# Down projections with six and seven seven-product blocks instead of five and five

## The chip, the cores and the metric

One core of a Trainium2 chip runs the whole program. The metric is the device time of one execution in microseconds. Before the change three runs took 2659.90, 2660.24 and 2660.72 us; the median is 2660.24.

## The reference

One decoder layer in float32 on 256 tokens of width 2048. It is a feed-forward part, a token mixer (a state-space branch and a windowed attention branch), and a second feed-forward part, each with a layer norm behind it:

```python
def swiglu(x, w_gate, w_up, w_down):
    return (jax.nn.silu(x @ w_gate) * (x @ w_up)) @ w_down

h = layer_norm(ALPHA * h + 0.5 * swiglu(h, ffn1_w_gate, ffn1_w_up, ffn1_w_down), ln1_g, ln1_b)
h = layer_norm(ALPHA * h + hybrid_mixer(h, ...), ln2_g, ln2_b)
h = layer_norm(ALPHA * h + 0.5 * swiglu(h, ffn2_w_gate, ffn2_w_up, ffn2_w_down), ln3_g, ln3_b)
```

The hidden width is 5632. The change touches the multiplication by `w_down` (5632 x 2048), which is done twice.

## The kernel before, in words

**Precision.** Every operand of a large product is split in two fp32r parts, high and low, and a product is three matmuls of 128 rows, 128 tokens and 512 columns: high by high, high by low, low by high (`three`, L900 to L904). The weights are split when they arrive: ScalarE copies a landed slab into `w_hi` (L1346), VectorE subtracts to get `w_lo` (L1795). A slab is two tiles of 128 weight rows by 512 columns, 512 KB. There are four landing buffers and four split buffers. SyncE issues the load of slab n when the low part of slab n-4 is done; ScalarE splits slab n when PE has finished slab n-4.

**The down projection.** The output's 2048 columns are done in two halves, j = 0 and 1, each of two column chunks c = 0 and 1. The 5632 rows are 22 k-pairs. Each half runs over the 22 pairs in `DOWN_ORDER[j]`, and each pair has one slab for each c; so a half has 44 slabs, numbered l = 0 to 43. An ordinary slab is 12 matmuls. The slabs of the next half go on counting as 44, 45 and so on in what follows. The projection of the first feed-forward part is "down 1" (f = 1), the other "down 2" (f = 2).

**Seven-product blocks.** For the pairs in `DOWN_SEVEN` the two slabs are multiplied as one 2x2 block product with seven products instead of eight: 21 matmuls instead of 24 (`seven_products`). For this a block needs
- mixed rows: four combinations of the tokens' tiles, in a tile of d_s[q] (high and low). VectorE adds and subtracts (`mixed_down`, L1987 to L1993), ScalarE makes the high part (L1456), VectorE the low part (`mixed_low`, L2019). They are made once, in the first half, and used in both halves;
- sums of the weights: four VectorE operations on the landed slabs (`block_sums`, L2027 to L2033), which need both slabs landed. ScalarE makes the high parts of the sums, VectorE their low parts (`t_low_parts`, L2039, L2042).

Products of a block go to two sets of four PSUM banks: the half's own banks, and the other half's banks (aux). When the last block of a half is done, ScalarE copies one aux bank (`copy_one_down`, L1532), and VectorE collects the rest into the residual (`collect_down`, L2117 to L2125). For j = 0 this stands at the start of the second half, ahead of its first slab's split, and PE waits for the banks; for j = 1 it stands ahead of slab 30 of that half. Own banks of the first half are evacuated at slabs 3 and 4 of the second (L2134, with statistics, L1849).

**Order.** Each engine runs its own list, written out slab by slab (`down` in the blocks of tensor, scalar and vector). In the first half VectorE also has, at slabs 10, 12, 14 and 16, the residual's rows: one operation each in down 1 (L2153), two of twice the length in down 2 (L1879, L1881, which read `rows`). Before the change the mixed tiles are made at slabs 11, 13, 15, 17 and 19, their low parts two slabs later, the blocks stand at slabs 22, 26, 30, 34 and 38 of the first half and 8, 12, 16, 20 and 24 of the second. The gains and biases of the last layer norm (`last_rows`, 2 MB) are loaded by GpSimd once PE has finished slab 23 of the second half of down 2; their place is that of pair 7, whose tiles lie where `last_rows` goes.

Of the kernel before, what the change touches and what calls it, by code (L numbers as in the profile page):

```python
# [26 lines left out]
P = 128  # L27
# [59 lines left out]
DOWN_SEVEN = (11, 13, 15, 17, 19)  # L87
DOWN_ORDER = (tuple(range(22)), (0, 1, 2, 3, 11, 4, 13, 5, 15, 6, 17, 7, 19, 8, 9, 10, 12, 14, 16, 18, 20, 21))
# [3 lines left out]
ALL_BLOCKS = UP_BLOCKS + 2 * len(DOWN_SEVEN)  # L92
# [110 lines left out]
def down_block(f, j, q):  # L203
    return (f - 1) * ALL_BLOCKS + UP_BLOCKS + j * len(DOWN_SEVEN) + q
# [68 lines left out]
def build_decoder_layer(nc, x, positions, ffn1_w_gate, ffn1_w_up, ffn1_w_down, ln1_g, ln1_b, w_in, conv_w, conv_b,  # L273
# [20 lines left out]
    with ctx:  # L294
# [15 lines left out]
        def placed(name, shape, dt, at):  # L310
# [72 lines left out]
               for k, at in enumerate((88, 92, 108, 112, 116))]  # L383
# [364 lines left out]
        def _(pe):  # L748
# [209 lines left out]
            def down_seven_block(f, j, l, own, aux):  # L958

                s = DOWN_ORDER[j][DOWN_SLABS[j][l][0]]  # L960
                q = DOWN_SEVEN.index(s)

                def rows_of(k, t):
                    return tuple(m[:, 2 * s + k, t * P:(t + 1) * P] for m in (g_hi, g_lo))

                if j == 0:
                    pe.wait_ge(mix_out, (f - 1) * MIXED + len(SEVEN) + q + 1)
                seven_products(down_block(f, j, q), slab_no(f"down{f}", j, l), l, l + 1, rows_of, d_s[q], "down",
                               own, aux, q == 0, q == len(DOWN_SEVEN) - 1)

            def down(f):

                for j in range(2):
# [5 lines left out]
                    for l, (p, c) in enumerate(DOWN_SLABS[j]):  # L979
                        if j == 1 and l >= 44 - HALVED:  # L980
                            break
                        if j == 0 and l == 3:
                            turn_hidden(f, NC_F - 1, (NC_F - 1) % 2)
                        s = DOWN_ORDER[j][p]
                        if s in DOWN_SEVEN:
# [351 lines left out]
        def _(act):  # L1337
# [189 lines left out]
            def copy_one_down(f, j):  # L1527

                act.wait_ge(t_used, down_block(f, j, len(DOWN_SEVEN) - 1) + 1)
# [4 lines left out]
            def down(f):  # L1534
                for j in range(2):
                    for l, (p, c) in enumerate(DOWN_SLABS[j]):
# [3 lines left out]
                        if j == 0 and l in (13, 15, 17, 19, 21):  # L1540
                            mixed_high(f, len(SEVEN) + (l - 13) // 2)
                        if (j, l) == (1, 0):
                            copy_one_down(f, 0)
                        if (j, l) == (1, 30):
                            copy_one_down(f, 1)
                        if s in DOWN_SEVEN and c == 1:
# [242 lines left out]
        def _(dve):  # L1789
# [216 lines left out]
            def mixed_down(f, q):  # L2006

                s = DOWN_SEVEN[q]
                if q == 0:
                    dve.wait_ge(gt_out, 2 * chunk_no(f, NC_F - 1))  # L2010
                    dve.wait_ge(t_rest, 2 * ((f - 1) * ALL_BLOCKS + UP_BLOCKS))
                at = slice(2 * s, 2 * s + 2)
# [126 lines left out]
            def down(f):  # L2139
                phase = f"down{f}"  # L2140
                for j in range(2):
                    for l, (p, c) in enumerate(DOWN_SLABS[j]):
# [23 lines left out]
                        if (j, l) == (1, 30):  # L2166
                            collect_down(f, 1)
                        n = down_block(f, j, DOWN_SEVEN.index(s)) if s in DOWN_SEVEN else None
                        if n is not None and c == 0:
                            dve.wait_ge(t_rest, n * 2)  # L2170
                            if s == DOWN_SEVEN[0]:
                                dve.wait_ge(mix_out, f * MIXED)
# [460 lines left out]
```

## Time and profile before

| | |
|---|---|
| median of 3 runs | 2660.24 us (2659.90 to 2660.72) |
| span of the profiled execution | 2657.8 us |
| PE | 2633.9 us busy, 99% |
| VectorE (DVE) | 1997.8 us busy, 75% |
| ScalarE (ACT) | 1371.5 us busy, 52% |
| down 1, first and second half | about 484 to 602 and 602 to 718 us |
| down 2, first and second half | about 2409 to 2526 and 2526 to 2642 us |
| HBM | 193 GB/s over the span |

The profile is of one execution; its span runs from its first to its last instruction, and the runs' times have some 2.4 us more. In the rows, L12 is line 12 of the kernel, PE is TensorE's matmul side, and a row such as "w_lo<-land,w_hi" names the tile written and the tiles read. A matmul's row shows 0.39 us because it contains the pipeline's latency; the distance between two starts is the time that one costs.

### The profile page before, as it was taken

How to read it: one execution, taken by the hardware profiler on the slowest of the kernel's cores; microseconds unless marked ns; L12 is line 12 of the kernel's file. 1: busy time of each engine (PE TensorE's matmuls, PEld its weight loads, DVE VectorE, ACT ScalarE, POOL GpSimd, SP SyncE). 2: the span in 40 equal slices, each digit the busy share in tenths (PEclk: the TensorE clock that was granted, in tenths of full speed). 3: DMA queues.
4: the chain of work that ended last, by engine and by line, in shares of the span. 5: the costliest groups of instructions: out<-in, count | busy, mean ns of one | idle time of the engine just before them, and what ended most of it. 6: DMA issues, size and time to landing. Idle time of an engine off the chain costs nothing.

```text
span 2657.8 us, 36761 instructions
## 1 busy us (share of the span) xinstructions
PE 2633.9 (99%) x12570; PEld 2187.7 (82%) x12570; DVE 1997.8 (75%) x2402; ACT 1371.5 (52%) x1710; POOL 129.6 (5%) x170
## 2 busy tenths in 40 slices
PE   9999999999999999999999999999999999999997
PEld 7888888888887788888888888888888888888886
DVE  6999997688666665677777765444789999977986
ACT  4555555455444554566555554444365555554553
POOL 1000000000000000211111100000000000000000
PEclk9999999999999999999999999999999999999999
DMA  7666666666655546665655565667666666666664
GB/s 224 199 197 202 193 198 213 211 201 196 204 173 148 153 150 198 206 181 180 179 177 174 180 180 166 190 190 248 203 209 198 194 206 192 202 204 230 209 208 171
DMA packets 286467, 513.96 MB, mean 193 GB/s; under 512 B 19664, under 2 KB 53120, under 8 KB 284320
## 3 DMA queue, kind: packets, MB, share of 16 engines
q1 hardware_dynamic: 279824, 485.03, 58.5%
q0 software_dynamic: 4880, 25.36, 2.6%
q10 hardware_dynamic: 1664, 2.26, 0.2%
q8 instruction: 61, 1.00, 0.2%
q14 instruction: 38, 0.31, 0.0%
HBM read 506.23 MB, written 6.36 MB: 193 GB/s over the span
## 4 chain that ended last, share of the span: by engine, by line
PE 95%; DVE 3%; ACT 1%; issue 0%; DMA 0%; ACTq 0%; POOLq 0%; POOL 0%; SPq 0%; DVEq 0%
PE acc L798 13%; PE acc L800 13%; PE acc L799 13%; PE acc L902 5%; PE acc L904 5%; PE acc L903 5%; PE acc L884 5%; PE acc L886 5%; PE acc L885 5%; PE spare L902 4%; PE spare L904 4%; PE spare L903 4%; PE spare L885 3%; PE spare L884 3%; PE spare L886 3%; PE spare L767 2%
## 5 line engine op out<-in xcount | busy, mean ns | idle before, releaser
L1795 DVE TENSOR_TENSOR w_lo<-land,w_hi 128x1024 fp32r<-128x1024 f32 (+1 forms) x956 | 1151.1, 1222 | 495.8 <-ACT w_hi L1346 488.0
L1346 ACT ACTIVATE w_hi<-land 128x1024 fp32r<-128x1024 f32 (+1 forms) x956 | 976.4, 1029 | 909.4 <-PE acc L800 324.1
L798 PE MATMUL acc<-w_hi,a_hi 128*128 128x512 f32 (+1 forms) x1168 | 443.9, 380 | 1.1 <-DVE w_lo L1795 1.1
L800 PE MATMUL acc<-w_hi,a_lo 128*128 128x512 f32 (+1 forms) x1168 | 428.8, 367 | 0.0
L799 PE MATMUL acc<-w_lo,a_hi 128*128 128x512 f32 (+1 forms) x1168 | 427.5, 366 | 0.0
L798 PEld LDWEIGHTS acc<-w_hi,a_hi 128*128 128x128 f32 x1168 | 220.3, 189 | 44.9 <-issue 10.1
L800 PEld LDWEIGHTS acc<-w_hi,a_lo 128*128 128x128 f32 x1168 | 220.2, 189 | 37.5
L799 PEld LDWEIGHTS acc<-w_lo,a_hi 128*128 128x128 f32 x1168 | 220.6, 189 | 36.5 <-issue 3.6
L884 PE MATMUL acc<-w_hi,a_hi 128*128 128x512 f32 x560 | 220.0, 393 | 0.7 <-DVE w_lo L1795 0.7
L886 PE MATMUL acc<-w_hi,a_lo 128*128 128x512 f32 x560 | 218.3, 390 | 0.0
L885 PE MATMUL acc<-w_lo,a_hi 128*128 128x512 f32 x560 | 217.8, 389 | 0.0
L884 PE MATMUL spare<-w_hi,a_hi 128*128 128x512 f32 x400 | 156.5, 391 | 0.0
L886 PE MATMUL spare<-w_hi,a_lo 128*128 128x512 f32 x400 | 155.7, 389 | 0.0
L885 PE MATMUL spare<-w_lo,a_hi 128*128 128x512 f32 x400 | 155.7, 389 | 0.0
L884 PEld LDWEIGHTS acc<-w_hi,a_hi 128*128 128x128 f32 x560 | 105.1, 188 | 23.0 <-DVE w_lo L1795 0.9
L886 PEld LDWEIGHTS acc<-w_hi,a_lo 128*128 128x128 f32 x560 | 105.1, 188 | 22.3
L885 PEld LDWEIGHTS acc<-w_lo,a_hi 128*128 128x128 f32 x560 | 105.2, 188 | 21.3
L902 PE MATMUL spare<-w_hi,g_hi 128*128 128x512 f32 x292 | 114.0, 390 | 0.6 <-DVE w_lo L1795 0.6
L902 PE MATMUL acc<-w_hi,g_hi 128*128 128x512 f32 x292 | 113.7, 389 | 0.0
L904 PE MATMUL spare<-w_hi,g_lo 128*128 128x512 f32 x292 | 113.6, 389 | 0.0
L904 PE MATMUL acc<-w_hi,g_lo 128*128 128x512 f32 x292 | 113.6, 389 | 0.0
L903 PE MATMUL spare<-w_lo,g_hi 128*128 128x512 f32 x292 | 113.6, 389 | 0.0
(393 smaller groups left out, 4302.7 us busy)
## 6 DMA issues: line engine op xcount, KB each, us to landing
land<-w_in SPq DMA_DIRECT2D x232, 512.0 KB, 3.8
land<-ffn_w_gate SPq DMA_DIRECT2D x176, 512.0 KB, 3.9
land<-ffn_w_up SPq DMA_DIRECT2D x176, 512.0 KB, 4.2
land<-ffn_w_down SPq DMA_DIRECT2D x176, 512.0 KB, 4.8
land<-w_ssd_o SPq DMA_DIRECT2D x64, 512.0 KB, 4.2
land<-w_in SPq DMA_DIRECT2D x132, 128.0 KB, 2.3
land<-w_attn_o SPq DMA_DIRECT2D x32, 512.0 KB, 4.2
land<-w_out SPq DMA_DIRECT2D x32, 512.0 KB, 4.5
```

The source lines that it names most:

```text
L767: return pe.transpose(spare[0:src.shape[-1], bank, at:at + rows], src, ident[0:rows, 0:rows])
L798: pe.matmul(to, rows_hi, hi, start=first, stop=False)
L799: pe.matmul(to, rows_hi, lo, start=False, stop=False)
L800: mm = pe.matmul(to, rows_lo, hi, start=False, stop=last)
L884: pe.matmul(to, rows_hi, hi, start=first and k == 0, stop=False)
L885: pe.matmul(to, rows_hi, lo, start=False, stop=False)
L886: mm = pe.matmul(to, rows_lo, hi, start=False, stop=last and k == 1)
L902: pe.matmul(to, rows[0], block[0], start=first, stop=False)
L903: pe.matmul(to, rows[0], block[1], start=False, stop=False)
L904: return pe.matmul(to, rows[1], block[0], start=False, stop=last)
L1346: act.activation(w_hi[:, l % SPLIT, 0:deep, 0:width], land[:, l % LAND, 0:deep, 0:width], ACT.Copy).then_inc(high, 1)
L1795: dve.tensor_tensor(w_lo[:, l % SPLIT, 0:deep, 0:width], land[:, l % LAND, 0:deep, 0:width], w_hi[:, l % SPLIT, 0:deep, 0:width].bitcast(F ...
```

## The change

Two more tiles of mixed rows are added. They don't fit into the region that the others lie in, so they have a buffer of their own (`d_more`, 8 KB of each partition), and the scratch for dynamic DMA is set to 4 KB. The blocks take pairs 10 to 15 in the first half and 10 to 16 in the second. In the first half they stand at slabs 20, 24, 28, 32, 36 and 40, in the second at 6, 10, 14, 18, 22, 26 and 30. Mixed tiles are made at slabs 9, 11, 13, 15, 17, 19 and (the seventh, for the second half alone) 42; low parts at 11, 13, 15, 17, 19, 20 and 43. The collecting of the second half moves from slab 30 to 36. The load of `last_rows` waits for slab 25 instead of 23, since pair 7 stands there now.

```diff
-DOWN_SEVEN = (11, 13, 15, 17, 19)
-DOWN_ORDER = (tuple(range(22)), (0, 1, 2, 3, 11, 4, 13, 5, 15, 6, 17, 7, 19, 8, 9, 10, 12, 14, 16, 18, 20, 21))
+DOWN_SEVEN = (10, 11, 12, 13, 14, 15, 16)
+DOWN_BLOCKS = (6, 7)
+DOWN_ORDER = ((0, 1, 2, 3, 4, 5, 6, 7, 8, 9, 10, 16, 11, 17, 12, 18, 13, 19, 14, 20, 15, 21),
+              (0, 1, 2, 10, 3, 11, 4, 12, 5, 13, 6, 14, 7, 15, 8, 16, 9, 17, 18, 19, 20, 21))
+DOWN_COLLECT = 36
+MIX_IN, MIX_HIGH, MIX_LOW = (9, 11, 13, 15, 17, 19, 42), (11, 13, 15, 17, 19, 20, 43), (11, 13, 15, 17, 19, 20, 43)
...
+def in_seven(j, s):
+    return s in DOWN_SEVEN[:DOWN_BLOCKS[j]]
...
-               for k, at in enumerate((88, 92, 108, 112, 116))]
+               for k, at in enumerate((88, 92, 108))]
+        d_more = sb("d_more", [P, 2, 2, 4, P], F32R)
+        d_s += [(d_more[:, k, 0, :, :], d_more[:, k, 1, :, :]) for k in range(2)]
+        d_s += [(placed(f"d_hi{k}", [P, 4, P], F32R, at * K), placed(f"d_lo{k}", [P, 4, P], F32R, (at + 2) * K))
+                for k, at in ((5, 112), (6, 116))]
...
-                        if j == 0 and l in (13, 15, 17, 19, 21):
-                            mixed_high(f, len(SEVEN) + (l - 13) // 2)
+                        if j == 0 and l in MIX_HIGH:
+                            mixed_high(f, len(SEVEN) + MIX_HIGH.index(l))
...
-                        if (j, l) == (1, 30):
+                        if (j, l) == (1, DOWN_COLLECT):
                             copy_one_down(f, 1)
...
+                if q == DOWN_BLOCKS[0]:
+                    dve.wait_ge(t_rest, 2 * down_block(f, 1, 0))
...
-                        if j == 0 and l in (11, 13, 15, 17, 19, 21):
-                            q = (l - 11) // 2
-                            if q > 0:
-                                mixed_low(f, len(SEVEN) + q - 1)
-                            if q < len(DOWN_SEVEN):
-                                mixed_down(f, q)
+                        if j == 0 and l in MIX_LOW:
+                            mixed_low(f, len(SEVEN) + MIX_LOW.index(l))
+                        if j == 0 and l in MIX_IN:
+                            mixed_down(f, MIX_IN.index(l))
...
-    nc = bacc.Bacc("TRN2", target_bir_lowering=False, num_devices=1)
+    nc = bacc.Bacc("TRN2", target_bir_lowering=False, num_devices=1, dynamic_dma_scratch_size=4096)
```

## Rows read from the trace of the kernel before

**Rows 1.** The page: busy time of PE, and the software DMA queue.
```profile
PE 2633.9 (99%) x12570; PEld 2187.7 (82%) x12570; DVE 1997.8 (75%) x2402; ACT 1371.5 (52%) x1710; POOL 129.6 (5%) x170
...
q0 software_dynamic: 4880, 25.36, 2.6%
```

**Rows 2.** Stretches: busy us (instructions) of PE, PEld, DVE, ACT, POOL; PE clock, DMA.
```profile
0.00:5.00 5.00, 2.39 (x10) 1.99 (x10) 0.00 (x0) 1.28 (x1) 3.91 (x49) 1.00 0.59 162
...
2440.00:2460.00 20.00, 19.45 (x86) 15.53 (x85) 19.45 (x27) 8.62 (x11) 0.00 (x0) 1.00 0.50 165
...
2643.00:2646.00 3.00, 0.00 (x0) 0.00 (x0) 2.46 (x7) 0.00 (x0) 1.52 (x2) 0.75 0.00 0
```

**Rows 3.** The chain of waits, 2400 to 2500 us: start, us, what.
```profile
2454.57 1.15 DVE w_lo L1795
2455.76 0.50 PE spare L902
```

**Rows 4.** PE in order of time: the first matmuls of blocks, and of slab 44.
```profile
545.26 0.39 PE L902 MATMUL acc<-w_hi,g_hi 128*128 128x512 f32 x1
...
2469.50 0.39 PE L902 MATMUL acc<-w_hi,g_hi 128*128 128x512 f32 x1
...
2510.30 0.39 PE L902 MATMUL acc<-w_hi,g_hi 128*128 128x512 f32 x1
...
2525.94 0.39 PE L902 MATMUL acc<-w_hi,g_hi 128*128 128x512 f32 x1
```

**Rows 5.** VectorE in order of time, down 2, splits of slabs 9, 11, 19.
```profile
2426.29 1.23 DVE L1795 TENSOR_TENSOR w_lo<-land,w_hi 128x1024 fp32r<-128x1024 f32 x1 [1.49 <-ACT w_hi L1346]
...
2431.09 0.68 DVE L1987 TENSOR_TENSOR sz<-g_hi,g_lo 128x512 f32<-128x512 f32 x1
...
2432.80 1.22 DVE L1795 TENSOR_TENSOR w_lo<-land,w_hi 128x1024 fp32r<-128x1024 f32 x1
...
2437.59 0.69 DVE L2019 TENSOR_TENSOR d_lo<-sz,d_hi 128x512 fp32r<-128x512 f32 x1
2438.31 0.69 DVE L1987 TENSOR_TENSOR sz<-g_hi,g_lo 128x512 f32<-128x512 f32 x1
...
2459.20 2.35 DVE L1795 TENSOR_TENSOR w_lo<-land,w_hi 128x1024 fp32r<-128x1024 f32 x2
```

**Rows 6.** VectorE, down 2, the first block (slab 22) up to the second.
```profile
2464.63 0.69 DVE L2027 TENSOR_TENSOR sz<-land 128x512 f32<-128x512 f32 x1 [1.34 <-DMA land<-ffn_w_down]
...
2467.42 2.35 DVE L1795 TENSOR_TENSOR w_lo<-land,w_hi 128x1024 fp32r<-128x1024 f32 x2
2469.69 1.22 DVE L2039 TENSOR_TENSOR d_t_lo<-sz,d_t_hi 128x1024 fp32r<-128x1024 f32 x1
...
2471.43 2.35 DVE L1795 TENSOR_TENSOR w_lo<-land,w_hi 128x1024 fp32r<-128x1024 f32 x2
2474.54 0.69 DVE L2027 TENSOR_TENSOR sz<-land 128x512 f32<-128x512 f32 x1 [0.77 <-DMA land<-ffn_w_down]
```

**Rows 7.** VectorE, down 1: slab 19's split, and the last block's sums.
```profile
531.16 1.22 DVE L1795 TENSOR_TENSOR w_lo<-land,w_hi 128x1024 fp32r<-128x1024 f32 x1
...
579.86 0.69 DVE L2027 TENSOR_TENSOR sz<-land 128x512 f32<-128x512 f32 x1 [1.42 <-DMA land<-ffn_w_down]
```

**Rows 8.** The copies into d_parts: ns min/median/max, first and last start.
```profile
L1532 ACT ACTIVATE d_parts<-acc x2: 599/600/600, 591.0 to 2515.3; 128x512 f32<-128x512 f32 x2
```

**Rows 9.** VectorE, down 2: collecting to slab 44's split, and an evacuation to the next split.
```profile
2516.44 0.68 DVE L2117 TENSOR_TENSOR d_parts<-d_parts,acc 128x512 f32<-128x512 f32 x1
...
2521.85 2.36 DVE L1795 TENSOR_TENSOR w_lo<-land,w_hi 128x1024 fp32r<-128x1024 f32 x2
...
2525.71 1.22 DVE L2134 SCALAR_TENSOR_TENSOR resid<-spare,resid 128x1024 f32<-128x1024 f32 x1
...
2528.28 1.23 DVE L1795 TENSOR_TENSOR w_lo<-land,w_hi 128x1024 fp32r<-128x1024 f32 x1
```

**Rows 10.** DMA issues, 2588 to 2594.6 us: count, KB each, median us to landing.
```profile
land<-ffn_w_down SPq DMA_DIRECT2D x4, 512.0 KB, 9.9
```

More of the change, by code:

```diff
@@ L91 @@
 UP_BLOCKS = NC_S * len(SEVEN)
-ALL_BLOCKS = UP_BLOCKS + 2 * len(DOWN_SEVEN)
+ALL_BLOCKS = UP_BLOCKS + sum(DOWN_BLOCKS)
 MIXED = len(SEVEN) + len(DOWN_SEVEN)
@@ L203, in down_block @@
 def down_block(f, j, q):
-    return (f - 1) * ALL_BLOCKS + UP_BLOCKS + j * len(DOWN_SEVEN) + q
+    return (f - 1) * ALL_BLOCKS + UP_BLOCKS + j * DOWN_BLOCKS[0] + q
+def in_seven(j, s):
+    return s in DOWN_SEVEN[:DOWN_BLOCKS[j]]
 def is_zero(n):
@@ L964, in rows_of @@
                     return tuple(m[:, 2 * s + k, t * P:(t + 1) * P] for m in (g_hi, g_lo))
-                if j == 0:
-                    pe.wait_ge(mix_out, (f - 1) * MIXED + len(SEVEN) + q + 1)
+                pe.wait_ge(mix_out, (f - 1) * MIXED + len(SEVEN) + q + 1)
                 seven_products(down_block(f, j, q), slab_no(f"down{f}", j, l), l, l + 1, rows_of, d_s[q], "down",
-                               own, aux, q == 0, q == len(DOWN_SEVEN) - 1)
+                               own, aux, q == 0, q == DOWN_BLOCKS[j] - 1)
             def down(f):
@@ L984, in down @@
                         s = DOWN_ORDER[j][p]
-                        if s in DOWN_SEVEN:
+                        if in_seven(j, s):
                             if s == DOWN_SEVEN[0] and c == 0:
@@ L1527, in copy_one_down @@
             def copy_one_down(f, j):
-                act.wait_ge(t_used, down_block(f, j, len(DOWN_SEVEN) - 1) + 1)
+                act.wait_ge(t_used, down_block(f, j, DOWN_BLOCKS[j] - 1) + 1)
                 if j == 1:
@@ L1539, in down @@
                             hidden_high(f, NC_F - 1, (NC_F - 1) % 2)
-                        if j == 0 and l in (13, 15, 17, 19, 21):
-                            mixed_high(f, len(SEVEN) + (l - 13) // 2)
+                        if j == 0 and l in MIX_HIGH:
+                            mixed_high(f, len(SEVEN) + MIX_HIGH.index(l))
                         if (j, l) == (1, 0):
                             copy_one_down(f, 0)
-                        if (j, l) == (1, 30):
+                        if (j, l) == (1, DOWN_COLLECT):
                             copy_one_down(f, 1)
-                        if s in DOWN_SEVEN and c == 1:
+                        if in_seven(j, s) and c == 1:
                             n = down_block(f, j, DOWN_SEVEN.index(s))
@@ L2165, in down @@
                             evacuate_down(f, 0, l - 3)
-                        if (j, l) == (1, 30):
+                        if (j, l) == (1, DOWN_COLLECT):
                             collect_down(f, 1)
-                        n = down_block(f, j, DOWN_SEVEN.index(s)) if s in DOWN_SEVEN else None
+                        n = down_block(f, j, DOWN_SEVEN.index(s)) if in_seven(j, s) else None
                         if n is not None and c == 0:
@@ L2171, in down @@
                             if s == DOWN_SEVEN[0]:
-                                dve.wait_ge(mix_out, f * MIXED)
+                                dve.wait_ge(mix_out, (f - 1) * MIXED + len(SEVEN) + DOWN_BLOCKS[j])
                             block_sums(phase, j, l, n)
```

## The prediction

> **What bounds the kernel now.** I read the page first: TensorE is busy for 99% of the span [rows 1], so only fewer matmuls, or fewer and shorter gaps between them, can move the time. Then the stretches of the second down projection: between 2440 and 2460 us PE is busy 19.45 of 20.00 us, and VectorE is busy for exactly as long; here the two engines are level, and PE has a gap [rows 2]. The chain of waits says who made it: a VectorE w_lo split leads to a late matmul at 2455.76 [rows 3]. So the down projections have a spare engine in PE's favour almost everywhere, but at the start of their seven-product blocks there is nothing left over. I then read PE's and VectorE's own lists in order of time, because the question is how far VectorE is ahead of PE slab by slab.
>
> The units, all from starts. PE: from the block at slab 22 to the one at slab 38 are four pairs of a block (21 matmuls) and an ordinary pair of slabs (24): 40.80 us for 180 matmuls, 0.2267 us each [rows 4]. A block is then 4.76 us, an ordinary slab 2.72, block and pair together 10.20. VectorE [rows 5, 6]: making a mixed tile 1.71 (2431.09 to 2432.80), its low part 0.72 (2437.59 to 2438.31), two splits 2.27 (2467.42 to 2469.69), so 1.14 one, 1.22 until its result can be used; the four sums of a block 2.79 (2464.63 to 2467.42); its two low parts of t 1.74 (2469.69 to 2471.43). Block and pair together are 2.79 + 2.27 + 1.74 + 2.27 = 9.07, and with the wait for the next slabs to land one such round takes 9.91 us (2464.63 to 2474.54). I take 10.0, since that round ends in a 0.77 us wait for DMA. VectorE gains 0.2 us a round on PE, no more.
>
> **Removed.** Ten blocks per down projection become 13 (6 and 7 instead of 5 and 5). Each new one saves one product of three matmuls: 3 x 0.2267 = 0.68 us; six of them in the two projections save 4.08 us. All of it is on PE, the path that sets the end. This is the most that the change can give, 0.15% of the time.
>
> The Trainium skill, TensorE: Matmul & The Clock Gate, Back-to-back issue gap, gives about 131 ns for a matmul of 512 columns in a stream with its weight loads. Eighteen matmuls would then be worth 2.4 us by an estimate from that page. The trace has 0.2267 us for these fp32r matmuls, and the sum goes by the trace.
>
> **The first block, two slabs earlier (down 2).** Before slab 20 six mixed tiles must now be ready, where five were needed by slab 22. The first of them goes ahead of slab 9's split, into VectorE's 1.49 us of idle time [rows 5]: 1.71 - 1.49 = 0.22 us late at most; I worked with 0.12, since the splits start 0.1 us after ScalarE's end anyway. The resid rows and the other tiles stand where they stood, but each low part comes two slabs sooner, so one more is done before slabs 16 to 19: +0.72. VectorE is 0.84 us later there, and as slab 17 was already what PE waited for, PE is 0.84 later from slab 17 on: 2456.60. It reaches slab 20 three slabs on, at 2464.76. VectorE starts slab 19's split at 2459.20 + 0.84 = 2460.04 [rows 5]; then split 1.14, low part of the sixth tile 0.72, sums 2.79, split of slab 20 1.22: 2465.91. PE is held another 1.15. Before, PE was at slab 20 at 2469.50 - 5.44 = 2464.06, and VectorE had the block ready without a gap. So **1.85 us** are lost. Bounds: 1.2, if the earlier shift is absorbed, to 2.6, if the loads of slabs 20 and 21 add a wait like the 1.34 us before the first sums now.
>
> **The same place in down 1** has lighter resid rows. VectorE starts slab 19's split at 531.16 [rows 7]; split, low part, sums and split end at 531.16 + 1.14 + 0.72 + 2.79 + 1.22 = 537.03, and PE is at slab 20 at 545.26 - 5.44 = 539.82 [rows 4]. Nothing is lost; 2.8 us of cover remain.
>
> **The turn from the first half to the second.** This is the dearest step. Collecting the first half (five VectorE operations and the splits behind them) stands ahead of slab 44's split. It needs the last block finished by PE and ScalarE's copy of one bank: the copy starts 5.0 us after that block's first matmul (2515.3 against 2510.30) and takes 0.60, so VectorE can start at +5.6 [rows 4, 8]. Then 5.41 us of collecting (2516.44 to 2521.85) [rows 9] and 1.22 for the split: slab 44 is ready at +12.23. Now the last block is at slab 38, four more ordinary slabs follow, and PE comes to slab 44 at +15.64 (2510.30 to 2525.94). After the change the last block is at slab 40 with only two ordinary slabs behind it: PE comes at 4.76 + 5.44 = +10.20. It must wait **at least 2.0 us, in both projections**. That holds whatever VectorE's lead is; the cover of two slabs (5.44 us) is gone.
>
> If VectorE is itself late it is more. From the sums of the last block it needs 2.79 + 2.27 + 1.74 = 6.80, the seventh mixed tile 1.71, split 1.14, its low part 0.72, split 1.14: it starts collecting 11.5 us after those sums. In down 2 the first sums start at 2461.90, five rounds of 10.0 later the last ones at 2511.9, collecting at 2523.4, slab 44 ready at 2530.05, PE there at 2465.91 + 51.00 + 10.20 = 2527.11: **2.9 us**, from 2.0 to 3.6 for rounds of 9.8 to 10.15. In down 1 the last block's sums now start at 579.86 [rows 7], 6.2 us ahead of PE's 545.26 + 40.80 = 586.06; with a lead of 5.9 or more only the 2.0 remain. The lead starts smaller after the change (539.82 - 533.02 = 6.8 instead of 8.4) and could fall to 4.2, which makes 3.7. I take **2.3**, near the row.
>
> **The second half.** After the turn PE starts slab 44 1.27 us after the collecting ends and reaches the first block, at slab 50, 17.6 us after it. VectorE has six splits (6.8) and two evacuations with statistics (2.57 each, 2525.71 to 2528.28) [rows 9], 12.0 in all, then 4.01 to the first usable split: 1.6 us to spare, growing by 0.2 a round. No loss there; 0 to 1.0 if rounds take 10.4. The late collecting keeps its six slabs behind the last block (36 after 30, as 30 after 24), and eight slabs are left behind it, 21.8 us in which VectorE has little to do. The end of the kernel is unchanged.
>
> **last_rows.** The 2 MB issued by GpSimd wait for slab 25 of the last half instead of 23. Now four weight loads of that stretch take 9.9 us each [rows 10], behind the last block and under ample lead. After the change one more block follows, and its second slab's load is under way when they start, with 2.6 us of VectorE's lead to live on. I add **0.3**, from 0 to 2.3 (landing 8.4 us after issue).
>
> The Trainium skill, DMA: Bandwidth & Descriptors, Issuing engines are not separate DMA queues, says that DMAs of different engines run on the same 16 DMA engines and interleave. The 9.9 us beside the 4.77 us that the load before the second sums of down 2 can have taken at most (2469.77 to 2474.54) agree; by that rule the moved load is a cost, and it is rival C's.
>
> **Smaller edits.** The two new tiles only change addresses. The smaller scratch serves the software queue, which carries 4880 packets in the whole span [rows 1]; none of its loads is near a deadline in the down projections: nothing, at worst 1 us. The first matmul after the gap took 0.50 us where the others have 0.39 [rows 3, 4]; for four gaps that and the restart make **0.2** (0 to 0.5).
>
> **Sum.** -4.08 + 1.85 + 2.3 + 2.9 + 0.3 + 0.2 = +3.5 us. The profiled execution spans 2657.8 us, the runs' median is 2660.24, 2.4 more for what lies around the span; the difference carries over: a span of 2661.3, and a time of **2663.7 us**, 0.13% slower.
>
> **Rivals.** About 0.2%, 5.3 us, is what a measurement can tell from no change, so faster means under 2654.9 and slower over 2665.6.
> A: the waits are hidden, since VectorE's lead absorbs them. Then 2660.24 - 4.08 = 2656.2. For it: in down 1 VectorE idles ahead of several splits. Against it: at the turn it is not lead but order, PE's last block to ScalarE's copy to VectorE. Chance 8%.
> B: only the turns cost (2 x 2.0), the first block is absorbed: 2660.2. Chance 22%.
> C: VectorE and the loads set the pace of the last half. With rounds of 10.6 us the 1.6 us to spare are used up in four rounds of 0.4, two more cost 0.8 in each projection, and the crowded load of the last block costs 2.3: 2663.7 + 1.6 + 2.0 = 2667.3. It decides once rounds exceed 10.4. For it: the wait for landing before nearly every block now. Against it: the 9.91 us round when VectorE is pressed. Chance 13%.
> D: PE's clock falls in a gap of 3 us. At the start it kept 1.00 over 5 us with only 2.39 us of PE work, and after the last matmul it was 0.75, then between its two levels [rows 2]. Each us at 1.2 GHz instead of 2.4 costs 0.5; ten of them 5: 2668.7. Chance 3%.
> The forecast has the other 54%, 2661.5 to 2665.5.
>
> **Chances and range.** Faster is out of reach by the sum, since even all 4.08 us stay within 5.3: 0.03 for something unseen. Slower takes C, D and a little of the forecast's upper end: 0.17. Same 0.80. The range from 2658.8 to 2666.4 leaves out most of A and half of C and D.
>
> **What would show it.** 18 matmuls fewer; 26 d_t tiles instead of 20; in both projections a PE gap of 2 to 3 us ahead of slab 44, waiting for w_lo, with the collecting starting 5.6 us (down 1) and 6.5 us (down 2) after the last block's first matmul; in down 2 gaps before slabs 17 and 20 that sum to 1.85 us above now; no gap in either second half. The prediction is wrong if PE has no gap at the turns, or if gaps stand before the blocks of the second half.

## The result, and the profile after

The changed kernel takes 2668.68 us (median of seven runs, 2665.95 to 2670.04) against 2660.14 (seven runs, 2659.89 to 2661.12) for the kernel before on the same chip: 8.5 us or 0.30% slower, ratio 1.003 with a 95% interval of 1.0021 to 1.004. A second set of seven, taken with the last experiments, gives 2668.08 (2666.42 to 2670.32) and 1.003 [1.0018, 1.0041]. The forecast of 2663.7 had the sign right, and the time lies above its range. Three executions of the experiments' sets took far longer, 3334 and 5401 us of the kernel before and 5397 us of one changed version (e9), and are left out of every figure.

The page of the changed kernel, the lines that answer to [rows 1]:

```profile
PE 2636.6 (99%) x12552; PEld 2187.0 (82%) x12552; DVE 2031.5 (76%) x2458; ACT 1379.5 (52%) x1726; POOL 128.6 (5%) x170
...
q0 software_dynamic: 4880, 25.36, 2.6%
```

Eighteen matmuls fewer, as the change says, and yet PE is busy 2.7 us longer. A busy figure that rises while the work falls suggests that some matmuls became slower. The waits say where PE stood. Of PE's waits in the changed kernel (total us, times, longest), these are on the down projections' line:

```profile
PE acc L914 <- DVE w_lo L1806: 6.1, 3, 2.6
...
PE spare L914 <- DVE w_lo L1806: 1.2, 2, 0.6
```

PE in order of time has these five waits: two in down 2 before slabs 16 and 17, one before the block at slab 20, and one at each turn (the first slab of the second half). In the kernel before there was only the 2455.76 of [rows 3]. The last block of the first half starts at 2522.59, 13.2 us ahead of slab 44 ([rows 4] had 15.64):

```profile
604.52 0.47 PE L914 MATMUL acc<-w_hi,g_hi 128*128 128x512 f32 x1 [2.37 <-DVE w_lo L1806]
...
2458.17 0.50 PE L914 MATMUL spare<-w_hi,g_hi 128*128 128x512 f32 x1 [0.63 <-DVE w_lo L1806]
...
2461.76 0.50 PE L914 MATMUL spare<-w_hi,g_hi 128*128 128x512 f32 x1 [0.53 <-DVE w_lo L1806]
...
2471.26 0.47 PE L914 MATMUL acc<-w_hi,g_hi 128*128 128x512 f32 x1 [1.04 <-DVE w_lo L1806]
...
2535.81 0.47 PE L914 MATMUL acc<-w_hi,g_hi 128*128 128x512 f32 x1 [2.64 <-DVE w_lo L1806]
...
2537.03 0.61 PE L916 MATMUL acc<-w_hi,g_lo 128*128 128x512 f32 x1
2537.43 0.63 PE L914 MATMUL acc<-w_hi,g_hi 128*128 128x512 f32 x1
2537.86 0.63 PE L915 MATMUL acc<-w_lo,g_hi 128*128 128x512 f32 x1
...
2539.99 0.61 PE L914 MATMUL acc<-w_hi,g_hi 128*128 128x512 f32 x1
2540.42 0.41 PE L915 MATMUL acc<-w_lo,g_hi 128*128 128x512 f32 x1
```

The last rows hold what I had not counted. 1.2 us after PE restarts, its matmuls start 0.43 us apart instead of 0.23, for eight of them, and then come back. The stretches of the same profile show what that is (columns as in [rows 2]):

```profile
0.00:5.00 5.00, 2.39 (x10) 1.99 (x10) 0.00 (x0) 1.28 (x1) 3.90 (x49) 1.00 0.58 162
2440.00:2460.00 20.00, 19.37 (x85) 15.52 (x85) 19.42 (x26) 7.50 (x9) 0.00 (x0) 1.00 0.45 138
...
600.00:604.00 4.00, 2.15 (x10) 1.46 (x8) 3.86 (x5) 2.12 (x2) 0.00 (x0) 1.00 0.30 94
604.00:608.00 4.00, 3.48 (x9) 2.75 (x10) 3.97 (x5) 0.00 (x0) 0.00 (x0) 0.64 0.52 143
2532.00:2536.00 4.00, 1.36 (x7) 0.85 (x6) 3.90 (x5) 1.35 (x2) 0.00 (x0) 1.00 0.14 55
2536.00:2540.00 4.00, 4.00 (x13) 3.11 (x13) 3.97 (x5) 0.00 (x0) 0.00 (x0) 0.63 0.68 202
2540.00:2544.00 4.00, 4.00 (x18) 3.29 (x17) 3.93 (x5) 1.84 (x2) 0.00 (x0) 0.94 0.76 262
```

The granted clock is 1.00 through each gap and falls to its lower level, 1.2 GHz, when PE is already back at work: 0.64 and 0.63 are means of a stretch with both levels. The 4 us after the second gap hold thirteen matmuls, where the same stretch at full clock holds eighteen or nineteen.

VectorE at the first block of down 2, answering to [rows 5, 6] (slab 19's split, the sixth tile's low part, the block's sums, the split of slab 20, and on to the next sums):

```profile
2465.19 1.22 DVE L1806 TENSOR_TENSOR w_lo<-land,w_hi 128x1024 fp32r<-128x1024 f32 x1
2466.32 0.68 DVE L2032 TENSOR_TENSOR d_lo<-sz,d_hi 128x512 fp32r<-128x512 f32 x1
2467.10 0.69 DVE L2040 TENSOR_TENSOR sz<-land 128x512 f32<-128x512 f32 x1
...
2469.89 2.35 DVE L1806 TENSOR_TENSOR w_lo<-land,w_hi 128x1024 fp32r<-128x1024 f32 x2
...
2477.05 0.69 DVE L2040 TENSOR_TENSOR sz<-land 128x512 f32<-128x512 f32 x1 [0.80 <-DMA land<-ffn_w_down]
```

There is no idle time between these four: VectorE itself is late, as forecast, and the round that follows takes 9.95 us (2467.10 to 2477.05).

VectorE's side of the second turn, answering to [rows 9] and [rows 8]:

```profile
2529.02 0.68 DVE L2130 TENSOR_TENSOR d_parts<-d_parts,acc 128x512 f32<-128x512 f32 x1
...
2534.43 2.36 DVE L1806 TENSOR_TENSOR w_lo<-land,w_hi 128x1024 fp32r<-128x1024 f32 x2
...
L1543 ACT ACTIVATE d_parts<-acc x2: 577/588/600, 596.8 to 2527.8; 128x512 f32<-128x512 f32 x2
```

Collecting takes 5.41 us, as before, and slab 44's split stands behind it; PE has run out of slabs at 2533.0.

To sum up the traces I took, for each stretch, the time between starts of matmuls beyond 0.2267 us each (the short 128x128 transposes by the identity left out):

| stretch of the changed kernel, us | before | after |
|---|---|---|
| 480 to 602, down 1 up to its turn (with the gap) | 0.09 | 2.83 |
| 602 to 717, the rest of down 1 | 0.08 | 1.93 |
| 2400 to 2530, down 2 up to its turn | 1.12 | 3.71 |
| 2530 to 2655, the rest, with the gap | -0.02 | 4.72 |

That is 11.92 us more, less 4.08 saved: 7.84 of the 10.44 by which the last matmul starts later (2652.43 against 2641.99). The other 2.6 lie outside the down projections: 0.75 within the first 12 us, where matmuls come at about half the rate until 11.2 us instead of 9.4, 0.87 at the restart after the first layer norm (a wait of 1.17 against 0.30 us), and small waits. They vary between executions of unchanged code: the second profile of the changed kernel has 0.45 at the start, e1, which changes nothing there, has the slow start until 11.3 us, and the experiments' profiles have waits of 0.3 to 1.1 us at that restart, or none.

### The profile page after: what moved, and what is told of

Same layout as the page of the kernel before. It is cut to its first block and busy times, and to the rows that moved or that the text cites. A ratio compares the mean times of both kernels' runs of the same rounds, so it can differ in the third digit from the quotient of the medians.

```text
span 2668.2 us, 36825 instructions
## 1 busy us (share of the span) xinstructions
PE 2636.6 (99%) x12552; PEld 2187.0 (82%) x12552; DVE 2031.5 (76%) x2458; ACT 1379.5 (52%) x1726; POOL 128.6 (5%) x170
## 5 line engine op out<-in xcount | busy, mean ns | idle before, releaser
L914 PE MATMUL acc<-w_hi,g_hi 128*128 128x512 f32 x266 | 105.2, 396 | 6.1 <-DVE w_lo L1806 6.1
L916 PE MATMUL acc<-w_hi,g_lo 128*128 128x512 f32 x266 | 104.9, 394 | 0.0
```

Of the source, the lines that this page charges most:

```text
L914: pe.matmul(to, rows[0], block[0], start=first, stop=False)
L916: return pe.matmul(to, rows[1], block[0], start=False, stop=last)
```

## Experiments

Ratios are to the kernel before, run on the same chip. The chip was another one for e1 to e4, e5 to e8, e9 to e12 and e13 to e15, so times of different groups compare less closely than the ratios do. A "fall" is a stretch in which the granted clock goes to its lower level.

### Scratch alone

```diff
-    nc = bacc.Bacc("TRN2", target_bir_lowering=False, num_devices=1)
+    nc = bacc.Bacc("TRN2", target_bir_lowering=False, num_devices=1, dynamic_dma_scratch_size=4096)
```

> The kernel before with nothing changed but the 4 KB of scratch for dynamic DMA. Of the 8.5 us that the change cost, the profile places some 8 in the two down projections and some 2.5 outside them (0.75 in the first 13 us, 0.9 in the first slabs after the first down projection, the rest in small steps). Theory 1: what lies outside is scatter of the loads' landing and has nothing to do with the scratch: 2660.1 us, at most 0.5 away. Theory 2: the smaller scratch (and the addresses that move with it) slows loads issued by GpSimd or what runs beside them: 2662 to 2663 us, with the later PE start after the first 13 us in the profile again.

Measured 2660.04 us (11 runs, 2659.52 to 2661.70), 1.000 [0.9991, 1.0009]. The scratch costs nothing that can be told.

### The turn: the first split ahead of the collecting

```diff
-                        if (j, l) == (1, 0):
+                        if (j, l) == (1, 1):
                             copy_one_down(f, 0)
...
-                        if (j, l) == (1, 0):
+                        if (j, l) == (1, 1):
                             collect_down(f, 0)
```

> The changed kernel, with slab 44's split put ahead of ScalarE's copy and VectorE's collecting at the turn of each down projection. Theory 1 (the order at the turn makes the gap, and the clock falls only because the gap is there): no gap in down 1 (at most 0.2 us), some 1.2 us in down 2 where VectorE itself is late, the clock at 1.00 around both turns; saved are 2.5 + 1.7 us in down 1 and 1.5 + 1.8 us in down 2, so about 2661 us. Rival (PE waits for the banks or for the loads as well, and the order only hides that): gaps of 2 us or more stay, 2666 us or more. Rival on the clock (it falls in these stretches whatever the gap): the gaps go, the clock still reads below 0.8 for some 4 us, about 2664.5 us.

Measured 2669.63 us (7 runs, 2662.47 to 2676.58), 1.0032 [1.0018, 1.0046]. In the profile both turns are nearly free (no gap in down 1, 0.98 us in down 2) and the clock stays at 1.00 around them, so the order was their cause; in this Theory 1 holds. Its time, 2661, does not. But what was won went elsewhere: 0.77 us at 649.02 (around the fourth block of the second half), and in this execution 4.58 us at the last block. VectorE's rows and the DMA issues around it name the cause:

```profile
2608.84 0.69 DVE L2040 TENSOR_TENSOR sz<-land 128x512 f32<-128x512 f32 x1 [6.71 <-DMA land<-ffn_w_down]
```

```profile
land<-ffn_w_down SPq DMA_DIRECT2D x6, 512.0 KB, 5.1
last_rows<-ln_g POOLq DMA_DIRECT2D x1, 1024.0 KB, 7.8
last_rows<-ln_b POOLq DMA_DIRECT2D x1, 1024.0 KB, 10.5
```

The 2 MB of last_rows were issued in these 15 us (2585 to 2600), and the next two weight loads took 9.7 us. The sums of the last block waited 6.71 us for one of them. That is rival C's collision, at twice its price, and a fall of 6.83 us comes on top of it, begun 2.5 us before PE restarts. It seems not to happen in every execution: 2662.47 to 2676.58 is a spread of 14 us, where the kernel before has 4; only the one execution was profiled.

### Gaps without blocks

```diff
                             collect_down(f, 0)
+                            for _ in range(6 if f == 1 else 7):
+                                ch.link(dve.tensor_tensor(d_parts[:, 0, :], d_parts[:, 1, :], d_parts[:, 2, :],
+                                                          ALU.add))
```

> The kernel before, with idle VectorE additions (128x512, 0.72 us each) behind the collecting at the turn, ahead of slab 44's split: six in down 1, seven in down 2. The cover now is 3.15 and 2.87 us, so they open PE gaps of about 1.2 us (down 1) and 2.2 us (down 2) in a kernel that has none of the changed order. Theory 1 (the clock's fall belongs to the gap's length; 1.04 us left it alone, 2.37 brought it down): the first gap leaves the clock at 1.00; the second is near the edge and shows which side 2.2 us is on. Time 2660.1 + 3.4 = 2663.5 us with no fall, 2665.3 us with one. Rival (the fall comes from what the changed kernel does beside the gap): no fall at either.

Measured 2665.64 us (11 runs, 2664.94 to 2668.86), 1.0022 [1.0013, 1.0031]. The gaps were 1.57 and 2.88 us (1.82 and 3.12 with the restart), and 2660.1 + 4.9 is 2665.1: the gaps alone explain the profiled execution, which took 2665.17. They are longer than the 1.2 and 2.2 us expected, and e14, the same program, has 0.94 and 2.20; so what the other ten executions held, gaps of this length or a fall, their times (2664.94 to 2668.86) do not tell. Behind the longer gap of this one the clock stays:

```profile
2528.00:2532.00 4.00, 1.12 (x6) 0.64 (x5) 3.90 (x5) 1.06 (x1) 0.00 (x0) 1.00 0.00 0
2532.00:2536.00 4.00, 4.00 (x19) 3.33 (x18) 3.97 (x5) 0.38 (x1) 0.00 (x0) 1.00 0.79 243
```

So the fall does not follow from a gap's length alone: 2.88 us had none here, 2.37 and 2.64 had one in the changed kernel.

### Blocks of five and seven

Five blocks in the first half, where the first one stands at slab 22 as before and the turn keeps its cover, and seven in the second; the two extra tiles are mixed in the second half.

```diff
-DOWN_BLOCKS = (6, 7)
+DOWN_BLOCKS = (5, 7)
+LATE_MIX = {8: 5, 12: 6}
...
-DOWN_ORDER = ((0, 1, 2, 3, 4, 5, 6, 7, 8, 9, 10, 16, 11, 17, 12, 18, 13, 19, 14, 20, 15, 21),
+DOWN_ORDER = ((0, 1, 2, 3, 4, 5, 6, 7, 8, 9, 15, 10, 16, 11, 17, 12, 18, 13, 19, 14, 20, 21),
...
+                        if j == 1 and l in LATE_MIX:
+                            dve.wait_ge(t_rest, 2 * (down_block(f, 1, (l - 8) // 4) + 1))
+                            mixed_down(f, LATE_MIX[l])
```

> Blocks five and seven: the first half is as in the kernel before (blocks at slabs 22 to 38), the second half is the changed one (blocks at slabs 6 to 30), and the two additional mixed tiles are made in the second half, at slabs 8 and 12 with their low parts a slab later. Two blocks more per down projection save 4 x 0.68 = 2.7 us. Theory 1 (all losses are in the first block and the turn, none in the second half): no new gap, 2660.1 - 2.7 = 2657.4 us. Rival (the second half with seven blocks costs by itself, VectorE or the loads setting its pace): gaps before its later blocks, 2660 us or more.

Measured 2664.70 us (11 runs), 1.0011 [1.0003, 1.002]. The profiled execution is the fastest, 2658.37, with no gap in the down projections but the old one (0.55 us at 2455.65). Four runs are at 2658.4 to 2659.6, one at 2661.4 and six at 2664.7 to 2667. The gaps are cured, as Theory 1 has it, and something that neither theory names adds 6 us in half of the executions; none of these was profiled. e6 and e11 look for it.

### last_rows four slabs later

```diff
-            pool.wait_ge(used, slab_no("down2", 1, 2 * DOWN_ORDER[1].index(7) + 1) + 1)
+            pool.wait_ge(used, slab_no("down2", 1, 29) + 1)
             load_rows(last_rows, ln3_g, ln3_b, last_rows_in)
```

> The changed kernel, but GpSimd's 2 MB load of last_rows waits until slab 29 of the last half is used instead of slab 25, so that the load of the last block's second slab is under way before it starts. Theory 1 (the load collides with the weight loads of the last block in some executions, and that makes the spread of 2665.95 to 2670.04): 2666 to 2667.5, the executions within 1.5 us of each other. Theory 2 (the collision is no matter for this kernel; its time is all gaps at the first block and the turns and TensorE's slow stretches behind them): 2668 to 2669, spread as before. If the later load is itself late for the end of the kernel, it is over 2670.

> The kernel of blocks of five and seven products, which had executions near 2659 and others near 2666, with the same later last_rows load (slab 29 of the last half). Theory 1 (the two groups are the collision of that load with the loads of the slab of the last block, or not): one group only, 2657 to 2659. Theory 2 (the two groups come from something else, such as a fall of TensorE's clock that a small gap can set off): still two groups, median 2661 to 2665.

The changed kernel: 2669.43 us (6 runs, 2666.69 to 2671.24), 1.0034 [1.0022, 1.0046]; its profile has the same gaps and both falls (Theory 2). The loads still meet the 2 MB, with a median of 11.0 us for the six issued between 2612 and 2622 us, and no gap comes of it. So in the changed kernel the collision is not what costs, though loads are slow in its first profile too, with the wait at slab 25: issues 2604 to 2611 us, answering to [rows 10].

```profile
land<-ffn_w_down SPq DMA_DIRECT2D x3, 512.0 KB, 9.0
```

Five and seven: 2665.41 (11 runs, 2658.14 to 2668.63), 1.0018 [1.0009, 1.0027], no better. The profile shows that the collision was only moved. PE in order of time, and the DMA issues 2600 to 2612 us:

```profile
2620.03 0.39 PE L917 MATMUL acc<-w_hi,g_lo 128*128 128x512 f32 x1
2623.95 0.50 PE L915 MATMUL acc<-w_hi,g_hi 128*128 128x512 f32 x1 [3.53 <-DVE w_lo L1809]
```

```profile
land<-ffn_w_down SPq DMA_DIRECT2D x5, 512.0 KB, 9.6
last_rows<-ln_g POOLq DMA_DIRECT2D x1, 1024.0 KB, 7.6
last_rows<-ln_b POOLq DMA_DIRECT2D x1, 1024.0 KB, 10.2
```

Weight loads take 9.6 us instead of about 4.5 (the median of those issued in 2540 to 2580 us of the kernel before). ScalarE waits 6.55 us for one of them, VectorE's collecting stands behind the split that is late by it, and PE's next slab behind the collecting. Slab 29 was the wrong place, not a test of none. My expectation of 2657 to 2659 failed for that.

### The residual's rows earlier

With the load at slab 29, and:

```diff
-                        if j == 0 and l in (10, 12, 14, 16):
-                            at = (2, 3, 0, 1)[(l - 10) // 2]
+                        if j == 0 and l in (6, 8, 10, 12):
+                            at = (2, 3, 0, 1)[(l - 6) // 2]
```

> The changed kernel with the later last_rows load, and with the residual rows of the second down projection (normalised and split off) prepared at slabs 6, 8, 10 and 12 instead of 10, 12, 14 and 16, before the mixed tiles crowd VectorE. Theory 1 (the first block is late only because VectorE does that work between the mixed tiles): no gap before slab 20 in either projection, 3.0 us less than the changed kernel with the later load alone, the turns unchanged at 2.4 and 2.6: 2663 to 2664.5. Theory 2 (the loads of the slabs, not VectorE's own work, make the first block late): the gaps stay, 2666 to 2668.

Measured 2666.88 us (7 runs, 2666.37 to 2671.75), 1.0029 [1.0018, 1.004]. The gap before slab 20 is gone, but three of 0.56, 0.64 and 0.56 us stand earlier, at 2443.10, 2446.75 and 2450.33; together with their restarts 2.68 us, against 3.05. The median is 2.5 us under e5's, of which the two profiles show 0.4 here, 0.5 at the turns and 0.7 at a small wait before 2528 that e5 has. VectorE now waits for its rows:

```profile
2423.23 1.23 DVE L1890 SCALAR_TENSOR_TENSOR resid<-resid,rows 128x1024 f32<-128x1024 f32 x1 [3.77 <-DMA rows<-ln_b]
```

Neither theory is whole. Moving VectorE's own work took the gap before slab 20 away, but at the earlier slabs the rows have not landed yet. Both turns have a fall here too.

### All at once

The early rows, last_rows at slab 29, the first split ahead of the collecting, and the seventh tile mixed at slab 8 of the second half.

> The changed kernel with four edits at once: the residual rows earlier, the later last_rows load, the collecting of the first half one slab behind its first split, and the seventh tile mixed in the second half at slab 8 instead of the first. All 18 matmuls stay saved. Theory 1 (the whole loss is order on VectorE, and the collision): no gap over 1 us in either down projection, 2656 to 2657.5, faster than the kernel before by 3 to 4 us. Theory 2 (VectorE has nothing left over in the second half of blocks of seven, so that what is taken off the turn comes back as gaps at the blocks around slabs 10 to 18): 2660 to 2663, with gaps of 0.5 to 1.5 us there.

Measured 2668.42 us (6 runs, 2665.96 to 2671.24), 1.0033 [1.002, 1.0045]: theory 2, and worse. PE in order of time:

```profile
623.07 0.50 PE L915 MATMUL acc<-w_hi,g_hi 128*128 128x512 f32 x1 [0.38 <-DVE w_lo L1809]
...
650.05 0.47 PE L915 MATMUL spare<-w_hi,g_hi 128*128 128x512 f32 x1 [0.55 <-DVE w_lo L1809]
...
2621.48 0.50 PE L915 MATMUL acc<-w_hi,g_hi 128*128 128x512 f32 x1 [1.26 <-DVE w_lo L1809]
...
2628.02 0.80 PE L915 MATMUL acc<-w_hi,g_hi 128*128 128x512 f32 x1 [3.53 <-DVE w_lo L1809]
```

The turns are free, and gaps stand among the blocks instead. The last one has the same form and length as e6's, with the load of last_rows at the same slab, and here the clock falls, 0.5 us before PE restarts. With six and seven blocks VectorE has little time left over to move things into, and the wait at the turn was, it seems, partly the recovery of its lead; four edits at once do not show which of them cost what.

### Filling the gap

```diff
                         pe.wait_ge(aux_out, shared_down(f, 0) + 1)
+                        for _ in range(9):
+                            pe.transpose(own[:, 0, 0:P], ident[:, :], ident[:, :])
```

> The changed kernel, with nine 128x128 transposes of the identity issued by TensorE at the turn of each down projection, between its wait for the collecting's last read of the banks and its wait for slab 44's w_lo. They take about 0.24 us each, 2.2 us together, inside a gap of 2.4 to 2.6 us that stays as long as it is; their results are overwritten. Theory 1 (the 1.69 and 1.8 us lost behind the gaps are TensorE's clock, which falls because it stood still): no slow matmuls behind either turn, 2665 to 2666, 3 us less than the changed kernel. Theory 2 (the slow matmuls come from the restart or from what else runs there, such as the loads): unchanged, 2668 to 2669.5. If the transposes themselves delay slab 44, it shows as 0.2 to 0.5 us more at each turn.

> The filled kernel, and the 2 MB load of last_rows waits until slab 37 of the last half is used, when nearly all weight loads are in. It must be there 15 us later, and lands 9 to 10.5 us after issue. Theory 1 (the load of last_rows costs something in some executions, wherever it meets weight loads): 0.5 to 2 us less than the filled kernel, and its executions within 1.5 us of each other. Theory 2 (no collision matters in the changed kernel): the same as the filled kernel within 0.5 us.

e9: 2665.92 us (11 runs, 2663.87 to 2667.22), 1.0018 [1.001, 1.0027], 2.2 to 2.8 us less than the changed kernel's two medians, of which one at least (e13's) is of another chip. e10: 2665.59 (11 runs, 2663.49 to 2669.26), 1.0019 [1.001, 1.0028], its Theory 2: last_rows makes no difference here. The stretches of e9 at both turns (busy of PE, clock, DMA):

```profile
602.20:606.00 3.80, 2.29 (x15) 1.00 0.03 10
606.00:610.00 4.00, 4.00 (x19) 1.00 0.82 258
2531.30:2535.30 4.00, 2.49 (x16) 1.00 0.08 12
2535.30:2539.30 4.00, 4.00 (x19) 1.00 0.85 267
```

No slow matmul in either, nineteen in the 4 us behind each turn, and slab 44 as late as in the changed kernel (2.71 us over the stream at the second turn, 2.80 there). e10's profile has none either, behind 0.93 and 1.46 us without work. That is none at four turns, against five of six in the three profiles of the changed kernel with its turns as they are (the first one, e5, e13). Theory 1 fits: the same loads and the same restart, and no slow matmuls once PE does not stand still for over 2 us. The nine transposes took 1.20 us, not 2.2, so 1.51 us without work remained in each gap of e9. Whether it is the transposes or the shorter stillness that kept the clock, this run does not part; no gap under 2 us in the down projections had a fall in any profile.

### Five and seven, last_rows behind the weights

```diff
-            pool.wait_ge(used, slab_no("down2", 1, 29) + 1)
+            pool.wait_ge(used, slab_no("down2", 1, 37) + 1)
```

> The kernel of blocks of five and seven, with last_rows loaded only after slab 37 of the last half is used. With the wait at slab 25 its executions were near 2659 or near 2666, with the wait at slab 29 from 2658.1 to 2668.6, and there the profile had a gap of 3.53 us before slab 36, behind four weight loads of 9.6 us each. Theory 1 (all executions over 2660 are this collision and the clock fall behind it): one group, 2657 to 2658.5, faster than before by 0.1%. Theory 2 (another cause makes the slower group): still executions at 2665 or more.

Measured 2659.09 us (11 runs, 2658.07 to 2660.64; before 2660.4), 0.9994 [0.9985, 1.0003]. One group, none over 2660.64, where the wait at slab 25 or 29 gave 14 of 22 runs at 2664 or more. So the slower group goes with the place of this load; what made up its 6 us no profile shows, since e6's, with the 3.53 us gap and no fall, is of an execution of 2663.07. In this profile the 2 MB land in 6.4 and 8.3 us, and the weight loads in 5.4. Theory 1 holds for the one group, though its time is 0.6 us above the one expected. The version is 1.3 us under the kernel before, of the 2.72 us that its four extra blocks save, and that is less than can be told from nothing. It is the best of all, and 9 to 9.6 us better than the change.

### Longer gaps, and three repeats

> The kernel before, with seven and nine idle VectorE additions (0.7 us each) behind the collecting of the first half in down 1 and down 2, which makes TensorE wait 2.2 us at the first turn and 4.3 us at the second, all else as before. Theory 1 (a longer gap makes the clock fall the more surely): a fall behind the second gap in the profile, 2667 to 2669. Theory 2 (the fall does not go by the gap's length): no fall, 2666.5 to 2667, that is 2660.1 + 2.4 + 4.5 less 0.3.

> The changed kernel again. Theory 1 (at the turns of this kernel the clock falls nearly always): slow matmuls for about 3.4 us behind both turns again, 2667 to 2670. Theory 2 (it falls in some executions only): at least one of the turns without them, and that execution is 1.7 us or more below 2668.7.

> The kernel before with six and seven idle VectorE additions behind the collecting, again. The first profile had a gap of 1.57 us and one of 2.88 us, and no fall. Theory 1 (the outcome is fixed by the program): no fall, 2665 to 2666. Theory 2 (it varies by execution): a fall behind the 2.9 us gap in this one, 2667 or more.

> The kernel before with seven and nine idle VectorE additions, again. The first profile had gaps of 1.66 and 3.11 us and a fall behind the second. Theory 1 (fixed by the program): a fall behind the second gap, 1.5 us, and none behind the first. Theory 2 (varies by execution): another pattern.

e12 (the edit of e3 with 7 and 9 additions): 2668.29 us (6 runs, 2666.55 to 2670.73), 1.0029 [1.0018, 1.0041]; gaps 1.66 and 3.11 us, a fall behind the second. e15, the same kernel: 1.66 and 3.12, a fall behind the second, 2667.69. The additions made shorter gaps than I had worked out (2.2 and 4.3 us), and both times the longer one had the fall: Theory 1 of e12 and of e15. e14: the kernel of e3, gaps 0.94 and 2.20, no fall, 2663.73; with its gaps 0.6 to 0.7 us shorter than in e3, it did not put the same question again. e13, the changed kernel again: a fall behind the gap of 2.02 us in down 1 and, with the same 2.64 us gap as in the first profile, none behind the second:

```profile
2532.00:2534.00 2.00, 0.00 (x0) 1.00 0.00 0
2534.00:2538.00 4.00, 3.95 (x18) 1.00 0.65 222
```

Theory 2 for e13 then: the same gap in the same program has a fall in one execution and none in another. That execution took 2666.42, the lowest of its seven. All profiles together, gaps in the down projections:

| gap, us | with a fall | without |
|---|---|---|
| under 2 us | none | all (up to 1.66) |
| 2.0 to 2.9 us | 2.02, 2.14, 2.37, 2.38, 2.41, 2.64, 2.64 | 2.20, 2.64, 2.88 |
| over 3 us | 3.11, 3.12, 3.53, 4.58 | 3.53 |

Each fall costs 1.5 to 2.1 us beyond its gap. Below 2.02 us there was no fall, and from there on the outcome varies by execution. The Trainium skill, TensorE: Matmul & The Clock Gate, What's actually happening, says that where the clock changes is not tied to the program's start, so that the count of slow matmuls differs from run to run; the traces agree, with a gap of 2.64 us at the same turn of the changed kernel, two executions with a fall and one without.

## Why the prediction was wrong

The step that failed is the clock: the sum has no term for slow matmuls behind the gaps that it forecasts. The clock stood as rival D, "PE's clock falls in a gap of 3 us", with 3%, at "each us at 1.2 GHz instead of 2.4 costs 0.5; ten of them 5: 2668.7". The mechanism is what happened, at both turns, for 3.4 us each: 1.85 us more in the rest of down 1, and 1.94 beyond the predicted-size gap in down 2, nearly all of it slow matmuls. The chance was wrong, and so was the price: D takes 5 us for ten at the lower level, where the two falls lasted 6.8 us and cost 3.8 with what stands around them. That D's 2668.7 is the measured median is luck; what the falls lack to it lies in small waits and outside the down projections. I took the first row of [rows 2], a clock of 1.00 over 5 us with 2.39 us of PE work, as evidence against. It is none. That 1.00 is no full speed, as the kernel before shows at its start, with the same four transposes once early and once late:

```profile
5.85 1.12 PE L767 MATMUL spare<-ident,resid 128*128 128x128 f32 x4 [1.74 <-DMA resid<-x]
...
9.59 0.60 PE L767 MATMUL spare<-ident,resid 128*128 128x128 f32 x4
```

Until 9.4 us such matmuls start 0.21 us apart, behind it 0.11, and the granted clock reads 1.00 over both. Twice the distance is what the lower level gives in the falls (0.425 against 0.2267), so the program seems to begin at that level, and the view does not say so. The row that did answer was in the same group: 0.75 over 2643 to 2646. The last matmul starts at 2641.99 and is over at 2642.4; a mean of 0.75 in 3 us is half of them at the lower level, so the clock fell at 2644.5, 2.1 us behind the last work. My own forecast had gaps of 2.3 and 2.9 us. Read that way, a fall at each turn was to be reckoned with in the forecast itself; what one costs, about 1.7 us, only the later profiles show. In the other profiles the clock falls between 2.0 and 5.3 us after the last matmul, and of the falls at gaps it comes 2.1 to 3.9 us after the last work, so one row alone does not settle it either.

The other steps, each against the profile of the changed kernel:

- **Removed, -4.08.** 18 matmuls fewer. Right.
- **First block of down 2, +1.85.** The two places of gaps now have 1.77 and 1.28 us over the stream, against 0.97 before: +2.1. In place they are right to 0.2 us. One of the gaps, before slab 16, stands a slab earlier than forecast. Down 2 begins 5.14 us later in the new profile; less that, slab 19's split starts at 2460.05 and PE restarts at 2456.6 and 2466.1, where 2460.04, 2456.60 and 2465.91 were worked out. With small waits the stretch has 2.6 more.
- **First block of down 1, 0.** No gap there. Right.
- **Turn of down 1, +2.3.** 2.53 with the restart. Right in the first profile, 2.18 in the second.
- **Turn of down 2, +2.9.** 2.80. Right, and e2 shows that the order of collecting and split makes it. The collecting starts 6.4 us after the last block's first matmul, where 6.5 was forecast, and 6.0 in down 1, where it was 5.6. Rival B is out.
- **Second half, 0.** No gap in the changed kernel, but less to spare than the 1.6 us worked out: with the turn's wait taken off, a gap of 0.77 us comes at a block of down 1 (e2), and more of them in e8, which also mixes the seventh tile there. By that the wait was covering them.
- **last_rows, +0.3.** Nothing measurable in the changed kernel (e5, e10). Rival C had the mechanism and not its bound: 2.3 us at most by my working, 4.58 us in e2, 3.53 in e6 and e8, which have another order or another place of the load, and a slower group of runs in the kernel of five and seven.
- **Scratch, 0.** e1.

So the sum is -4.08 + 2.6 + 2.7 + 2.8 + 3.8 = 7.8 in the down projections of the traced execution, 10.4 with what lies outside them, and 8.5 in the medians. That not every execution has both falls can be part of its spread (4.1 us, against 1.2 in the seven runs before), but this isn't shown: the kernel before has 4.0 in a larger set. Without the falls, e9 gives 2665.9, inside the forecast's range and still 2.2 over the forecast. The first block's small waits (0.7), the first turn (0.4) and waits outside the down projections account for that in part; the rest stays open. With a fall at each turn the forecast would have been 2663.7 + 3.4 = 2667.1, past the range's end of 2666.4; the range had to hold that as soon as the falls had an even chance.

## What to carry to other kernels

Where a gap of TensorE is forecast, ask in the same breath what the clock does behind it, and look at the end of the profile: how soon after the last matmul the granted clock falls is a sign of how long a gap can be without one. Take it from several profiles, since here it was 2.0 to 5.3 us; in the down projections no gap up to 1.66 us had a fall, and one of 2.02 had. Nine idle transposes in each gap, with slab 44 as late as before, made the kernel 2 to 3 us shorter, by themselves or by the shorter standstill that they leave. And before moving work off a wait, ask whether the wait is where the other engine regains its lead; here gaps came back at the blocks. A large load from another queue goes where few weight loads are left to meet, not a few slabs further on; in the kernel of five and seven that took the group near 2666 us away. And a granted clock of 1.00 at a program's start is to be checked against the distance between two matmuls.

## What was not expected of the hardware

- Behind gaps under 3 us the clock falls only when PE is back at work, 0.05 to 1.23 us after its restart. The second turn of the changed kernel, in finer stretches (busy of PE, clock, DMA):

```profile
2533.20:2535.80 2.60, 0.00 (x0) 1.00 0.00 2
2535.80:2536.80 1.00, 0.99 (x4) 1.00 0.16 14
2536.80:2540.40 3.60, 3.60 (x10) 0.53 0.80 248
```

- At gaps over 3 us it began inside the gap in three of four cases, 0.42 us (e12), 0.53 (e8) and 2.50 (e2) before the restart. e12:

```profile
2529.00:2531.70 2.70, 0.03 (x1) 1.00 0.00 0
2531.70:2532.10 0.40, 0.00 (x0) 0.52 0.00 0
```

- Ten of the eleven falls last 3.41 us (eight or so matmuls at 0.425 us instead of 0.2267), behind a gap of 2.02 us as behind those of 2.64; the one at e2's 4.58 us lasts 6.83.
- Nine 128x128 transposes of float32 took 1.20 us in the stream, where ten at the program's start took 2.39 us in the profile. The distance of two starts is 0.11 us there and 0.21 here. The larger distance lasts until about 9 to 11 us, by execution, and the view of the granted clock shows 1.00 all the while.
- Two loads of 1 MB beside 512 KB weight loads double the latter, from 4.5 to 9.6 us in e6, and land in 7.6 and 10.2 us themselves; with few weight loads left (e10) they land in 5.0 and 6.9.
